# The second pair row of one token tile, moved to GpSimd at the end of a two-layer trunk

## The chip, the cores and the metric

The kernel runs on one core of a Trainium2 chip. A core has a matrix engine (TensorE, PE in the profile), a vector engine (VectorE, DVE), a scalar engine (ScalarE, ACT), GpSimd (POOL) and SyncE (SP), which only issues transfers. Each engine works through its own queue of instructions in program order, and semaphores hold an instruction back until others have finished. The metric is the device time of one execution in microseconds (us), lower is better. A few runs of the same kernel lie between 996.86 and 999.53 us.

## What is computed

256 latent tokens and 256 context tokens of width 1024 pass through two layers; each has a mixer and a mixture of experts with 32 experts, of which every token uses two. In the second ("odd") layer only the latent tokens are computed to the end. The change touches the last step of that layer, the sum over the two experts of each token, and what follows it:

```python
# top-2 experts of the chosen group, weights top_w
def add_expert(acc, p):
    w1_e, w3_e, w2_e, c_e = p
    hidden = jax.nn.silu(t @ w1_e) * (t @ w3_e)
    return acc + c_e[:, None] * (hidden @ w2_e), None
...
x = x + mx[5] * hierarchical_moe(hx, *moe_p)     # mx[5]: the gate
return rmsnorm(x, norm_final)
```

For a token with experts a and b this is x + w_a·g·y_a + w_b·g·y_b, and then a norm over the row.

## The kernel before

**Experts.** The 32 experts run one after the other, each on up to 64 gathered token rows (CAP = 64). TensorE makes a hidden layer (L1256), turns it (L1266) and multiplies it down to 1024 columns (L1282), which stand in PSUM as two halves of 512 columns on 64 partitions each. In the odd layer VectorE multiplies the result by the gate into the tile `YS` (L2439, in RH), and GpSimd scatters the rows by an indirect transfer to `pair_out` in HBM (L2844). There every token has two rows, one for its first and one for its second expert.

**Late experts.** The results of the last two experts (`LATE`, 30 and 31) don't take the way through HBM in the odd layer. Their places in `pair_out` are filled with zeros early on, and TensorE adds their rows from `YS` to the tokens by a product with `late_T`, a table of weights built beforehand (L1380). The other results come back: when GpSimd has seen the scatters end, it raises `most_stored` (L2942), and SyncE issues four loads (L876) into `back[t]` (in RAB), one for each tile t of 128 tokens and half h of 512 columns. Each counts on its own semaphore `y_back[t][h]`. A load of 512 KB brings both rows of the 128 tokens, first at `D*h` and second at `D*h + 512`.

**The end of the odd layer.** `LATE_TILES = (1, 0)`: tile 1 goes first, tile 0 is the second late tile. For each tile, TensorE (`late_results`) runs four late products (two experts, two halves; L1380) and then, for each half, one product of `first_weight[:, t, :]`, a diagonal matrix of the first expert's weights, with the first rows in `back` (L1385); it closes the PSUM bank of that half. An f32 product appears in the profile as two or more records. VectorE (`late_pair`) adds for each half the second rows times `topw[:, t, 1:2]` to the state X (L2498), and then the closed bank to X (L2505), which raises `x_updated`. ScalarE takes squares of the updated X (L1764) and a root (L1768); VectorE forms the reciprocal (L2194) and the normalised rows (L2198), and ScalarE's queue stores them (L2111). The helper `step` makes an instruction count on a semaphore of its engine and lets what follows on this engine wait for it.

**Order.** The queues follow the program: on VectorE, tile 1's two L2498, its two L2505, tile 0's two L2498, its two L2505, then the two final tiles. GpSimd has nothing to do after `most_stored` in the odd layer.

Of the kernel before, what the change touches and what calls it, by code (L numbers as in the profile page):

```python
# [19 lines left out]
ALU = mybir.AluOpType  # L20
# [4 lines left out]
D = 1024  # L25
# [281 lines left out]
LATE = (EXPERTS - 2, EXPERTS - 1)  # L307
LATE_TILES = (1, 0)
# [29 lines left out]
def trunk(nc, A):  # L338
# [6 lines left out]
    with ctx:  # L345
        def sb(name, shape, dt=F32):
            return ctx.enter_context(nc.sbuf_tensor(name, shape, dt))

        def sem(name):
            return ctx.enter_context(nc.semaphore(name))  # L350


        X = sb("X", [P, 4, D])
# [76 lines left out]
        back = [RAB[:, 0:2048], RAB[:, 2048:4096], RH[:, 2048:4096], RM[:, 0:2048]]  # L430
# [38 lines left out]
        topw = small[:, 152:160].rearrange("p (t k) -> p t k", t=4)  # L469
# [82 lines left out]
        first_hot_ready, first_full, first_ready = sem("first_hot_ready"), sem("first_full"), sem("first_ready")  # L552
        extra_ready, routed = sem("extra_ready"), sem("routed")
        rows_sent = sem("rows_sent")
        gidx_ready, sidx_ready = sem("gidx_ready"), sem("sidx_ready")
        gathered = [sem(f"gathered{i}") for i in range(4)]
        scattered = [sem(f"scattered{i}") for i in range(2)]
# [13 lines left out]
        y_back = [[sem(f"y_back{t}{h}") for h in (0, 1)] for t in range(4)]  # L571
# [39 lines left out]
        def full(eng, *name):  # L611

            eng.wait_ge(psum_full, plan[name]["full"])
            return bank_of(name)

        def drained(eng, *name):

            job = plan[name]
            eng.wait_ge(act_drained if job["who"] == "act" else dve_drained, job["drained"])
# [65 lines left out]
        def gate_loaded(eng, l, v):  # L685
            eng.wait_ge(ld_gate[l, v], 16 * (2 - l))

        def chained(eng, semaphore):

            count = [0]  # L690

            def step(ins, wait=True):
                count[0] += 1
                ins.then_inc(semaphore, 1)
                if wait:
                    eng.wait_ge(semaphore, count[0])

            step.sync = lambda: eng.wait_ge(semaphore, count[0])
            step.lag = lambda n: eng.wait_ge(semaphore, count[0] - n)
            return step  # L700
# [242 lines left out]
        def _(pe):  # L943
# [3 lines left out]
            def open_bank(*name):  # L947
                assert next(order) == name, name
                for before in plan[name]["before"]:
                    drained(pe, *before)  # L950
                return bank_of(name)

            def close(mm):
                mm.then_inc(psum_full, 1)
# [6 lines left out]
            def freed(mm):  # L961

                if free_due[0]:
                    mm.then_inc(ring_free, free_due[0])
                    free_due[0] = 0
# [243 lines left out]
            def experts(l):  # L1209
# [161 lines left out]
                def late_results():  # L1371

                    banks = {(t, h): open_bank("late", l, t, h) for t, h in LATE_BANKS}
                    pe.wait_ge(late_ready, l + 1)
                    for t in LATE_TILES:
                        for e, expert in enumerate(LATE):
                            pe.wait_ge(y_ready, n0 + expert + 1)
                            for h in (0, 1):
                                p = slice(CAP * h, CAP * (h + 1))
                                mm = pe.matmul(banks[t, h], late_T[p, t, e, :], YS[p, expert % 2, :],  # L1380
                                               start=(e == 0), stop=False)
                                freed(mm)
                        for h in (0, 1):
                            pe.wait_ge(y_back[t][h], 16 * (l + 1))
                            close(pe.matmul(banks[t, h], first_weight[:, t, :], back[t][:, D * h:D * h + 512],  # L1385
                                            start=False, stop=True))
# [22 lines left out]
                with pe.Fori(PEELED[l], LAST_GROUP) as i:  # L1409
                    c = extra_counts(pe, l, i)  # L1410
                    for q in range(PER_LOOP):
                        step(i, q, c[q])
                last_steps(extra_counts(pe, l, LAST_GROUP))
                late_results()

                pe.wait_ge(y_ready, n0 + EXPERTS)
# [37 lines left out]
            for c in range(NCH):  # L1454
                g = c % 4
                mm = pe.matmul(bank[32 * g:32 * g + 32, 0:BLK], shift32[:, c, :], first_w[:, c, :],
                               start=(c < 4), stop=(c >= 4))
# [7 lines left out]
            for ft in (0, 1):  # L1465
                mm = pe.matmul(bank[:, 8 * ft:8 * ft + 8].rearrange("p (j s) -> p j s", j=4), shift_rows[:, P * ft:P * (ft + 1)],
                               ident.rearrange("p (j k) -> p j k", j=4)[:, :, 0:2], start=True, stop=True)
# [4 lines left out]
            for c in range(4):  # L1472
                mm = pe.transpose(bank[:, 40 * c:40 * c + 37], chan_rows[0:37, P * c:P * (c + 1)], ident[0:37, 0:37])
# [165 lines left out]
            in1 = {(what, b): at["in1", i] for i, (what, b, _) in enumerate(ODD_BLOCKS)}  # L1639
# [58 lines left out]
            for g in (0, 1):  # L1698
                bank = open_bank("DT", g)
                for n in range(4):  # L1700
                    pe.wait_ge(o_scaled, 4 * g + n + 1)
                    mm = pe.transpose(bank[:, P * n:P * (n + 1)], OD[:, 4 * g + n, :], ident)
# [412 lines left out]
        def _(dve):  # L2115
            step = chained(dve, dve_step)

            def done(ins):
                ins.then_inc(dve_drained, 1)
# [370 lines left out]
            def late_pair(l):  # L2490


                for t in LATE_TILES:
                    if l == 1:
                        for h in (0, 1):
                            half = slice(512 * h, 512 * (h + 1))
                            dve.wait_ge(y_back[t][h], 32)
                            step(dve.scalar_tensor_tensor(out=X[:, t, half], in0=back[t][:, D * h + 512:D * (h + 1)],  # L2498
                                                          scalar=topw[:, t, 1:2], in1=X[:, t, half],
                                                          op0=ALU.mult, op1=ALU.add))  # L2500
                    for h in (0, 1):
                        half = slice(512 * h, 512 * (h + 1))
                        bank = full(dve, "late", l, t, h)
                        if l == 1:
                            dve.tensor_tensor(X[:, t, half], X[:, t, half], bank, ALU.add).then_inc(x_updated, 1)  # L2505
                            continue
                        b = back[t][:, D * h + 512:D * (h + 1)]
                        dve.wait_ge(y_back[t][h], 16)
                        done(dve.scalar_tensor_tensor(out=b, in0=b, scalar=topw[:, t, 1:2], in1=bank,
                                                      op0=ALU.mult, op1=ALU.add))  # L2510
                        drained(dve, "late", 0, t, h)
                        gate_loaded(dve, 0, 5)
                        step(dve.tensor_tensor(b, b, G[:, t // 2, half], ALU.mult))
                        dve.tensor_tensor(X[:, t, half], X[:, t, half], b, ALU.add).then_inc(x_updated, 1)
# [158 lines left out]


            late_pair(0)
            for t in (1, 0):
                normed_tile(2, t)
# [110 lines left out]
        def _(pool):  # L2788
            step = chained(pool, pool_step)
# [24 lines left out]
            def experts(l):  # L2814
# [21 lines left out]
                def scatter(i, q):  # L2836
                    n, b = i * PER_LOOP + (n0 + q), q % 2
                    pool.wait_ge(y_ready, n + 1)
                    e = i * PER_LOOP + q
                    col = idx[:, 0, 1, e:e + 1] if isinstance(e, int) else idx[:, 0, 1, bass.ds(e, 1)]  # L2840
                    pool.tensor_copy(SIDX[b], col).then_inc(sidx_ready, 1)  # L2841
                    pool.wait_ge(sidx_ready, n + 1)
                    pool.sem_inc(pool_passed, 1)
                    pool.indirect_dma_start(out=pair_out[l], out_offset=bass.IndirectOffsetOnAxis(ap=SIDX[b], axis=0),  # L2844
                                            in_=YS[:, b, :], in_offset=None, bounds_check=4 * tokens[l] - 1,
                                            oob_is_err=False).then_inc(scattered[b], 16)
# [11 lines left out]
                def stored(x):  # L2858

                    with pool.If(x > 0):  # L2860
                        pool.wait_ge(x_scattered, x * 16)
# [78 lines left out]
                    pool.wait_ge(scattered[b], 16 * ((n0 + EXPERTS) // 2 - 1))  # L2940
                stored(pool.snap(extras))
                pool.sem_inc(most_stored, 1)  # L2942
                if l == 0:
                    for t in LATE_TILES:
                        for h in (0, 1):
                            pool.wait_ge(y_back[t][h], 16)
                    for q in (PER_LOOP - 2, PER_LOOP - 1):
                        scatter(LAST_GROUP, q)
                    for b in (0, 1):
                        pool.wait_ge(scattered[b], 16 * EXPERTS // 2)  # L2950
                    pool.sem_inc(pairs_stored, 1)
# [42 lines left out]
```

## Time and profile before

| | |
|---|---|
| median of 3 runs | 997.68 us (996.86 to 999.53) |
| the profiled execution, its time | 997.07 us |
| the profiled execution, its span in the trace | 995.3 us |
| TensorE busy, share of the span | 934.7 us, 94% |
| VectorE | 427.9 us, 43% |
| ScalarE | 247.2 us, 25% |
| GpSimd | 224.5 us, 23% |
| mean granted TensorE clock | 0.993 of full speed |

The profile comes from one execution; its own time is 1.8 us above the span of its instructions. Times in the rows below count from the span's start. The busy shares are means over all stages; the change lies in the last 14 us alone, and is read from there.

### The profile page before, as it was taken

What the parts mean: (1) busy time and instruction counts of PE and PEld (TensorE: products, weight loads), DVE (VectorE), ACT (ScalarE), POOL (GpSimd) and SP (SyncE); (2) the same over time, 40 slices, a digit from 0 to 9 for tenths busy, and PEclk for the clock granted to TensorE, in tenths of its full rate; (3) what the DMA queues carried; (4) which work ended last, traced back from release to release, by engine and by line L of the source; (5) the groups of instructions that cost most, each with busy time, mean ns of one, the idle gap of its engine ahead of it and who ended that gap; (6) DMA issues with size and microseconds to landing.
All of it is one profiled execution on the core that took longest, in us unless ns stands there. A gap on an engine that the chain in (4) does not pass through costs nothing.

```text
span 995.3 us, 17268 instructions
## 1 busy us (share of the span) xinstructions
PE 934.7 (94%) x5873; PEld 591.6 (59%) x5874; DVE 427.9 (43%) x906; ACT 247.2 (25%) x538; POOL 224.5 (23%) x309
## 2 busy tenths in 40 slices
PE   4999999999998899997988999999988999999986
PEld 3444448657886455554555565887875555555552
DVE  4399995577446011110111589556344222222224
ACT  4220102465243122221222340133143111111112
POOL 1017801110003333332431000000003343333310
PEclk9999999999999999999999999999999999999999
DMA  9979325899357899999999999883558999999996
GB/s 346 391 198 376 98 72 197 252 307 390 131 184 244 328 405 405 407 406 407 407 406 407 326 387 388 282 315 107 196 185 283 400 400 408 405 399 401 403 405 240
DMA packets 129948, 315.86 MB, mean 317 GB/s; under 512 B 28987, under 2 KB 60755, under 8 KB 129860
## 3 DMA queue, kind: packets, MB, share of 16 engines
q1 hardware_dynamic: 114152, 295.93, 79.9%
q0 software_dynamic: 10800, 12.72, 3.7%
q10 hardware_dynamic: 4908, 6.03, 1.7%
q8 instruction: 57, 0.93, 0.4%
q14 instruction: 31, 0.25, 0.1%
HBM read 315.00 MB, written 22.31 MB: 339 GB/s over the span
## 4 chain that ended last, share of the span: by engine, by line
PE 75%; DMA 12%; DVE 4%; issue 3%; SPq 2%; ACT 2%; POOLq 0%; DVEq 0%; POOL 0%; ACTq 0%
PE ps L1256 19%; PE ps L1056 17%; DMA ring<-in_moe_w 10%; PE ps L1282 9%; PE ps L1108 8%; PE ps L1066 6%; PE ps L1224 3%; PE ps L980 2%; PE ps L1266 2%; PE ps L1434 1%; DMA RH<-hrow,sidx_all 1%; SPq L765 1%; DMA mod_rows<-in_norm_ffn 1%; PE ps L1485 1%; PE ps L1516 1%
## 5 line engine op out<-in xcount | busy, mean ns | idle before, releaser
L1256 PE MATMUL ps<-ring,RT 128*64 128x256 f32 x2096 | 250.8, 387 | 17.3 <-DMA ring<-in_moe_w 14.8
L1256 PEld LDWEIGHTS ps<-ring,RT 128*64 128x64 f32 x2096 | 156.5, 139 | 84.4 <-issue 18.2
L1056 PE MATMUL ps<-RT,ring 128*128 128x512 f32 (+1 forms) x544 | 182.1, 493 | 1.1 <-DVE RT L2532 1.1
L1056 PEld LDWEIGHTS ps<-RT,ring 128*128 128x128 f32 x544 | 102.2, 190 | 77.2 <-issue 70.6
L2409 DVE TENSOR_TENSOR RT<-RT,ps 64x256 f32<-64x256 f32 x64 | 27.0, 423 | 257.1 <-ACT RT L1859 139.0
L1282 PE MATMUL ps<-ring,RT 128*64 128x512 f32 x424 | 100.3, 593 | 2.2 <-DVE RT L2415 1.8
L1859 ACT ACTIVATE RT<-ps 64x256 f32<-64x256 f32 x64 | 24.2, 378 | 242.9 <-PE ps L1256 221.9
L2579 DVE SCALAR_TENSOR_TENSOR RAB<-RM,chan,RAB 128x512 f32<-128x512 f32 x120 | 82.3, 766 | 0.0
L2844 POOL DMA_INDIRECT pair_out<-RH,sidx_all x62 | 63.2, 1019 | 55.4 <-POOL sidx_all L2841 51.7
L2820 POOL DMA_INDIRECT RH<-hrow,idx x7 | 7.8, 1120 | 288.6 <-DMA hrow<-RH 189.1
L2832 POOL DMA_INDIRECT RH<-hrow,sidx_all x56 | 59.3, 1060 | 49.4 <-issue 29.0
L1224 PEld LDWEIGHTS ps<-const,RH 128*128 128x128 f32 x252 | 35.0, 208 | 48.6 <-issue 48.6
L1853 ACT ACTIVATE RT<-ps 128x512 f32<-128x512 f32 x64 | 38.2, 597 | 74.1 <-PE ps L1224 70.0
L1066 PE MATMUL ps<-ring,RT 128*128 128x256 f32 x256 | 56.0, 380 | 0.0
L1282 PEld LDWEIGHTS ps<-ring,RT 128*64 128x64 f32 x424 | 31.3, 137 | 39.6 <-issue 30.7
L1066 PEld LDWEIGHTS ps<-ring,RT 128*128 128x128 f32 x256 | 48.5, 190 | 8.0 <-issue 1.6
L2415 DVE COPY RT<-ps 128x128 f32<-128x128 f32 x64 | 18.7, 291 | 75.9 <-PE ps L1266 70.4
L2958 POOL TENSOR_TENSOR RM<-RM,PR 128x512 f32<-128x512 f32 x4 | 33.6, 8421 | 71.8 <-ACT PR L1738 71.8
L1224 PE MATMUL ps<-const,RH 128*128 128x128 f32 x252 | 46.5, 307 | 2.2 <-issue 1.2
L2841 POOL COPY sidx_all<-idx 128x1 int32 (+1 forms) x62 | 11.5, 186 | 147.9 <-ACT RH L1868 67.3
L1108 PE MATMUL ps<-ring,RT 128*128 128x256 f32 x192 | 43.2, 381 | 0.9 <-ACT RT L1738 0.9
L1108 PEld LDWEIGHTS ps<-ring,RT 128*128 128x128 f32 x192 | 36.0, 190 | 7.2 <-issue 1.4
(325 smaller groups left out, 1061.6 us busy)
## 6 DMA issues: line engine op xcount, KB each, us to landing
ring<-in_moe_w SPq DMA_DIRECT2D x354, 512.0 KB
ring<-in_w_mod SPq DMA_DIRECT2D x96, 512.0 KB
ring<-in_odd_w_in SPq DMA_DIRECT2D x24, 512.0 KB
ring<-in_even_w_in SPq DMA_DIRECT2D x20, 512.0 KB
ring<-in_even_w_out SPq DMA_DIRECT2D x8, 512.0 KB
RAB<-in_moe_w SPq DMA_DIRECT2D x8, 512.0 KB, 7.4
RAB<-pair_out SPq DMA_DIRECT2D x8, 512.0 KB, 8.4
ring<-in_odd_w_out SPq DMA_DIRECT2D x8, 512.0 KB
```

The costliest lines, as they stand in the source:

```text
L1056: mm = pe.matmul(bank, w[:, c, P * ft:P * (ft + 1)], moving[:, c, :], start=(c == 0), stop=(c == NCH - 1))
L1066: mm = pe.matmul(bank[:, BLK * i:BLK * (i + 1)], chunk_of(c, t), w[:, c, :], start=(c == 0), stop=(c == NCH - 1))
L1108: mm = pe.matmul(bank[:, BLK * (b % 2):BLK * (b % 2 + 1)], source[:, c % 4, P * t:P * (t + 1)], w[b][:, c, :], start=(c == 0 and b % 2 == ...
L1224: mm = pe.transpose(ps[:, b, P * j:P * (j + 1)], XG[:, q % 4, j:512:4], ident)
L1256: mm = pe.matmul(bank[CAP * k:CAP * (k + 1), 0:BLK], xt(c), rows_at(w[k], c), start=(c == 0), stop=(c == NCH - 1))
L1282: mm = pe.matmul(bank[CAP * k:CAP * (k + 1), :], ht(f), w[:, D * f + 512 * k:D * f + 512 * (k + 1)], start=(f == 0), stop=(f == 1))
L1853: act.activation(XT[:, b, :, :, :].rearrange("p j a s -> p (j a s)"), ps[:, bank, :], ACT.Copy).then_inc(xT_ready, 1)
L2409: dve.tensor_tensor(HID[:, b, :], SA[:, b, :], ps[CAP:P, 2 + b, 0:BLK], ALU.mult).then_inc(hid_ready, 1)
L2579: return dve.scalar_tensor_tensor(out=out, in0=z, scalar=chan[:, ct, k:k + 1], in1=out, op0=ALU.mult, op1=ALU.add)
L2832: pool.indirect_dma_start(out=XG[:, q % 4, :], out_offset=None, in_=hrow[l], in_offset=bass.IndirectOffsetOnAxis(ap=GIDX[q % 4], axis=0), ...
L2844: pool.indirect_dma_start(out=pair_out[l], out_offset=bass.IndirectOffsetOnAxis(ap=SIDX[b], axis=0), in_=YS[:, b, :], in_offset=None, boun ...
L2958: pool.tensor_tensor(z, z, SG[:, ct % 2, :].rearrange("p (s t) -> p s t", s=2), ALU.mult).then_inc(gated_in, 1)
```

## The change

For tile 0 of the odd layer, and for nothing else:

- TensorE leaves out the two diagonal products; the late products of the last expert close the banks.
- GpSimd, after `most_stored`, waits for each half's load, multiplies the second rows in place by their weight and adds them to X; the addition raises the new semaphore `second_added`.
- VectorE's scaled addition (now L2508) takes the first rows (k = 0) in place of the second, and waits for `second_added` too.

Tile 1 stays as it was, and so does the even layer.

```diff
+        second_added = sem("second_added")
...
+                                last = (l, t) == (1, LATE_TILES[1]) and e == len(LATE) - 1
                                 mm = pe.matmul(banks[t, h], late_T[p, t, e, :], YS[p, expert % 2, :],
-                                               start=(e == 0), stop=False)
-                                freed(mm)
+                                               start=(e == 0), stop=last)
+                                if last:
+                                    close(mm)
+                                else:
+                                    freed(mm)
+                        if (l, t) == (1, LATE_TILES[1]):
+                            continue
                         for h in (0, 1):
                             pe.wait_ge(y_back[t][h], 16 * (l + 1))
                             close(pe.matmul(banks[t, h], first_weight[:, t, :], back[t][:, D * h:D * h + 512],
...
+                        k = 1 if t == LATE_TILES[0] else 0
                         for h in (0, 1):
                             half = slice(512 * h, 512 * (h + 1))
                             dve.wait_ge(y_back[t][h], 32)
-                            step(dve.scalar_tensor_tensor(out=X[:, t, half], in0=back[t][:, D * h + 512:D * (h + 1)],
-                                                          scalar=topw[:, t, 1:2], in1=X[:, t, half],
+                            if k == 0:
+                                dve.wait_ge(second_added, h + 1)
+                            step(dve.scalar_tensor_tensor(out=X[:, t, half], in0=back[t][:, D * h + 512 * k:D * h + 512 * (k + 1)],
+                                                          scalar=topw[:, t, k:k + 1], in1=X[:, t, half],
                                                           op0=ALU.mult, op1=ALU.add))
...
                 pool.sem_inc(most_stored, 1)
+                if l == 1:
+                    t = LATE_TILES[1]
+                    for h in (0, 1):
+                        half = slice(512 * h, 512 * (h + 1))
+                        pool.wait_ge(y_back[t][h], 32)
+                        second = back[t][:, D * h + 512:D * (h + 1)]
+                        step(pool.tensor_scalar(second, second, topw[:, t, 1:2], None, ALU.mult))
+                        pool.tensor_tensor(X[:, t, half], X[:, t, half], second, ALU.add).then_inc(second_added, 1)
```

At the end of TensorE's queue, after tile 1's late products, stood before (semaphores waited for in brackets; `y_back10` is tile 1, half 0):

```order
L1385 MATMUL ps<-RAB,BIAS 128x512 [waits y_back10]
L1385 MATMUL ps<-RAB,BIAS 128x512 [waits y_back11]
L1380 MATMUL ps<-RH,BIAS 128x512 [waits y_ready]
L1380 MATMUL ps<-RH,BIAS 128x512
L1380 MATMUL ps<-RH,BIAS 128x512 [waits y_ready]
L1380 MATMUL ps<-RH,BIAS 128x512
L1385 MATMUL ps<-RAB,BIAS 128x512 [waits y_back00]
L1385 MATMUL ps<-RAB,BIAS 128x512 [waits y_back01]
```

and now, with the diagonal products at L1392 and the late ones at L1382:

```order
L1392 MATMUL ps<-RAB,BIAS 128x512 [waits y_back10]
L1392 MATMUL ps<-RAB,BIAS 128x512 [waits y_back11]
L1382 MATMUL ps<-RH,BIAS 128x512 [waits y_ready]
L1382 MATMUL ps<-RH,BIAS 128x512
L1382 MATMUL ps<-RH,BIAS 128x512 [waits y_ready]
L1382 MATMUL ps<-RH,BIAS 128x512
```

Tile 0's two diagonal products are gone; nothing else on TensorE moved.

On VectorE, from tile 1's second scaled addition to the first final tile, stood before:

```order
L2498 SCALAR_TENSOR_TENSOR X<-RAB,small,X 128x512 [waits y_back11,dve_step]
L2505 TENSOR_TENSOR X<-X,ps 128x512 [waits psum_full,dve_step]
L2505 TENSOR_TENSOR X<-X,ps 128x512 [waits psum_full]
L2498 SCALAR_TENSOR_TENSOR X<-RAB,small,X 128x512 [waits y_back00]
L2498 SCALAR_TENSOR_TENSOR X<-RAB,small,X 128x512 [waits y_back01,dve_step]
L2505 TENSOR_TENSOR X<-X,ps 128x512 [waits psum_full,dve_step]
L2505 TENSOR_TENSOR X<-X,ps 128x512 [waits psum_full]
```

and now:

```order
L2508 SCALAR_TENSOR_TENSOR X<-RAB,small,X 128x512 [waits y_back11,dve_step]
L2515 TENSOR_TENSOR X<-X,ps 128x512 [waits psum_full,dve_step]
L2515 TENSOR_TENSOR X<-X,ps 128x512 [waits psum_full]
L2508 SCALAR_TENSOR_TENSOR X<-RAB,small,X 128x512 [waits second_added,y_back00]
L2508 SCALAR_TENSOR_TENSOR X<-RAB,small,X 128x512 [waits second_added,y_back01,dve_step]
L2515 TENSOR_TENSOR X<-X,ps 128x512 [waits psum_full,dve_step]
L2515 TENSOR_TENSOR X<-X,ps 128x512 [waits psum_full]
```

The instructions and their places are the same; tile 0's two scaled additions each wait for GpSimd as well.

GpSimd's queue ended with the wait for the scatters; behind it stands now:

```order
L2870 UNCONDITIONAL_BRANCH [waits x_scattered]
L2959 TENSOR_SCALAR RAB<-RAB,small 128x512 [waits y_back00]
L2960 TENSOR_TENSOR X<-X,RAB 128x512 [waits pool_step]
L2959 TENSOR_SCALAR RAB<-RAB,small 128x512 [waits y_back01]
L2960 TENSOR_TENSOR X<-X,RAB 128x512 [waits pool_step]
```

Four instructions are added there; each addition waits for the scaling ahead of it (`pool_step`).

## Rows read from the trace of the kernel before

**Rows 1.** Chain of work that ended last, the end: start us, us, what.

```profile
981.34 1.92 PE ps L1380 x8
983.26 1.91 PE ps L1385 x4
985.17 1.92 PE ps L1380 x8
987.09 1.93 PE ps L1385 x4
989.04 0.04 DVE X L2505
...
991.36 0.75 DVE RH L2198
```

**Rows 2.** Timeline of VectorE from 981 us: start, us, engine, line, operation, tiles, count.

```profile
981.99 1.53 DVE L2498 SCALAR_TENSOR_TENSOR X<-RAB,small,X 128x512 f32<-128x512 f32 x2
984.42 1.48 DVE L2505 TENSOR_TENSOR X<-X,ps 128x512 f32<-128x512 f32 x2 [0.90 <-PE ps L1385]
985.82 1.53 DVE L2498 SCALAR_TENSOR_TENSOR X<-RAB,small,X 128x512 f32<-128x512 f32 x2
988.25 1.48 DVE L2505 TENSOR_TENSOR X<-X,ps 128x512 f32<-128x512 f32 x2 [0.90 <-PE ps L1385]
```

**Rows 3.** Timeline of TensorE, its last two groups, tile 0.

```profile
985.11 1.99 PE L1380 MATMUL ps<-RH,BIAS 64*128 64x512 f32 x8
987.02 1.98 PE L1385 MATMUL ps<-RAB,BIAS 128*128 128x512 f32 x4
```

**Rows 4.** Timeline of ScalarE, the first squares of tile 0.

```profile
988.98 0.63 ACT L1764 ACTIVATE RAB<-X 128x512 f32<-128x512 f32 x1 [1.70 <-DVE X L2505]
```

**Rows 5.** Loads of L876, second and third, then third and fourth: starts, landing times.

```profile
L876 SPq DMA_DIRECT2D RAB<-pair_out x2: 431/432/434, 974.0 to 974.4; - x2
...
DMA to landing us min/median/max: 7.8/8.2/8.6
```

```profile
L876 SPq DMA_DIRECT2D RAB<-pair_out x2: 431/432/432, 974.4 to 974.9; - x2
...
DMA to landing us min/median/max: 8.6/9.0/9.3
```

**Rows 6.** Timeline of GpSimd: last instruction, then two-input additions, then one-input masks.

```profile
967.22 0.98 POOL L2844 DMA_INDIRECT pair_out<-RH,sidx_all  x1 [0.86 <-POOL sidx_all L2841]
```

```profile
61.90 4.31 POOL L2958 TENSOR_TENSOR RM<-RM,PR 128x512 f32<-128x512 f32 x2 [56.84 <-ACT PR L1738]
```

```profile
81.18 28.16 POOL L2958 TENSOR_TENSOR RM<-RM,PR 128x512 f32<-128x512 f32 x1 [14.97 <-ACT PR L1738]
```

```profile
109.30 1.18 POOL L2958 TENSOR_TENSOR RM<-RM,PR 128x512 f32<-128x512 f32 x1
110.43 0.45 POOL L2801 TENSOR_SCALAR_AFFINE_SELECT BIAS<-BIAS 64x288 f32<-64x288 f32 x1
111.03 0.45 POOL L2803 TENSOR_SCALAR_AFFINE_SELECT BIAS<-BIAS 64x288 f32<-64x288 f32 x1
```

```profile
112.23 0.71 POOL L2803 TENSOR_SCALAR_AFFINE_SELECT BIAS<-BIAS 64x288 f32<-64x288 f32 x1
...
154.34 2.50 POOL L2963 TENSOR_TENSOR RM<-RAB 128x512 f32<-128x512 f32 x2 [31.16 <-DVE RAB L2579]
```

**Rows 7.** Timeline of VectorE beside those GpSimd instructions.

```profile
59.39 7.90 DVE L2164 SCALAR_TENSOR_TENSOR RH<-ring,csilu,RH 128x1024 f32<-128x1024 f32 x5
```

```profile
78.40 29.90 DVE L2579 SCALAR_TENSOR_TENSOR RAB<-RM,chan,RAB 128x512 f32<-128x512 f32 x45
108.21 1.01 DVE L2143 SCALAR_TENSOR_TENSOR mod_rows<-ps,small,mod_rows 128x256 f32<-128x256 f32 x2
```

```profile
154.11 0.69 DVE L2603 TENSOR_TENSOR ps<-ps,BIAS 128x512 f32<-128x512 f32 x1
154.84 1.23 DVE L2604 TENSOR_REDUCE small<-ps 128x2 f32<-128x1024 f32 x1
```

**Rows 8.** Groups by line and shape on GpSimd: count, busy us, mean ns, idle before.

```profile
L2851 POOL MEMSET RH<- 128x512 f32 x2 | 1.1, 548 | 0.0
```

## Prediction

> **What bounds the kernel now.** I read the chain of work that ended last first, and only its end, since nothing before the loads of L876 is touched. From 981.34 us it runs through TensorE alone: late products of tile 1, its diagonal products, late products of tile 0, its diagonal products, about 1.92 us each, until VectorE adds the last bank to X [rows 1]. Then comes the tail: squares and root on ScalarE, reciprocal and scaled rows on VectorE, the store [rows 1, 4]. The timeline of VectorE says how much room there is beside that chain. Before each pair of L2505 it stood idle for 0.90 us with TensorE as releaser; tile 0's scaled additions ran from 985.82 to 987.35, and the bank addition had to wait until 988.25 [rows 2]. So the diagonal products of tile 0 sit on the path, and behind them VectorE has 0.90 us of slack, no more. GpSimd's last instruction ended at 967.22 + 0.98 = 968.2 us [rows 6]: it is free.
>
> **The change part by part.** *Removed:* tile 0's diagonal products, 1.98 us of TensorE [rows 3]. Their banks now close when the late products end, at 985.11 + 1.99 = 987.10 us [rows 3]. The full 1.93 us of the chain isn't the gain, because VectorE is late next: tile 0's scaled additions end at 987.35 at the earliest, and the bank addition then starts there in place of 988.25 [rows 2]. That caps the gain at 0.90 us. Everything behind (ScalarE's squares at 988.98, the two final tiles, the stores) hangs on tile 0's L2505 and moves with it one for one [rows 1, 4].
>
> *Unchanged in cost:* VectorE's two scaled additions of tile 0 read the first rows in place of the second, the same 128x512 shape from the same load, 1.53 us for two or some 0.75 us each [rows 2].
>
> *Added:* four GpSimd instructions in one queue, two scalings and two additions, and a wait of each of VectorE's two scaled additions for the GpSimd addition of its half. Queued behind that wait on VectorE are tile 0's bank additions and both final tiles, so nothing can go around it. GpSimd's own waits hold nobody else, as its queue ends there, and `most_stored` is raised ahead of them, so the loads start as before.
>
> When GpSimd can start: tile 0's loads are the third and fourth. The third was issued at 974.4 and landed 8.6 us later, at 983.0; the fourth at 974.9 and 9.3 us, at 984.2 [rows 5].
>
> What its instructions cost: the addition has rows of its own shape. Undisturbed it took 1.18 us, and 2.50 us for two, 1.25 each, beside VectorE instructions that take one input from SBUF or none [rows 6, 7]. I take 1.22. A scaling of 128x512 isn't in the trace. From below it is bounded by a memset of that shape, 0.55 us, which reads nothing [rows 8]; from above by the one-input mask of 288 columns in 0.45 us, which grows with the columns to 0.45 x 512 / 288 = 0.80 us [rows 6]. I take 0.65, in the middle. Between two GpSimd instructions of which the second waits for the first stand 111.03 - 110.88 = 0.15 us [rows 6]. So each half costs 0.65 + 0.15 + 1.22 = 2.02 us, and both 4.04 us.
>
> Where it meets VectorE: a GpSimd addition that began beside the convolution's scaled additions took 28.16 us; it ended at 109.34, 1.04 us after the run of 45 such VectorE instructions had at 108.30, which is about one addition's own time [rows 6, 7]. Those VectorE instructions have two inputs in SBUF, as L2498 has; the one that followed had one input in PSUM, as L2505 has, and didn't hold it up. Beside longer two-input instructions two additions took 4.31 us, 2.15 each [rows 6, 7]. So I count that the two engines exclude each other where VectorE runs a scaled addition, whichever began first, and not where it adds a bank.
>
> The Trainium skill says as much on the page "SBUF — State Buffer", section "Who interferes with whom": a VectorE instruction with two SBUF inputs and a GpSimd instruction that reads SBUF share one port pair, and the later one blocks until the first has finished. The trace bears it out with the 28.16 us; the rule speaks against this change, and with it the sum below comes to a loss, without it to a small gain (the second rival).
>
> The sum, in the trace's times. Load at 983.0, but VectorE is in tile 1's second scaled addition until 981.99 + 1.53 = 983.52 [rows 2]. GpSimd's first half: 983.52 + 2.02 = 985.54; VectorE's tile 1 additions of banks run beside it undisturbed to 985.90. GpSimd goes on with the scaling of half 1 from 985.54 to 986.19. VectorE, ready for tile 0's first scaled addition at 985.82 as before, finds the port taken, runs from 986.19 to 986.94, and now GpSimd's second addition, ready at 986.34, has to wait for it: 986.94 + 1.22 = 988.16. VectorE sees the semaphore some 0.04 us later and runs its second scaled addition to 988.95. The bank addition starts at about 988.97, against 988.25 before: **0.7 us later**.
>
> Ends of this sum: with scaling 0.80 and addition 1.25 the same steps give 985.72, 986.52, 987.27, 988.52, 989.31, a loss of 1.1 us. With a scaling of 0.55, an addition of 1.18 and a start at the load, the first half ends at 984.88, the second scaling at 985.43; if the second addition then takes the port ahead of VectorE it ends at 986.76, VectorE's two scaled additions follow to 988.26, and the loss is nothing. So 0.0 to 1.1 us later, and I take 0.7, which the middle values give. The cover for GpSimd's first half is TensorE's work on both tiles, which ends at 987.10; without that cover each further us of GpSimd would be a us of the end, as the second half's already is.
>
> Against the profiled execution: 997.07 + 0.7 = 997.8 us. Its time lies 0.6 us under the median of the runs shown, so the median becomes 997.68 + 0.7 = **998.4 us**.
>
> **The rivals.** *GpSimd and VectorE don't hold each other up here, or GpSimd is quick.* Then GpSimd runs through from 983.0: with 2.02 us each half it ends at 987.05, VectorE's second scaled addition at 987.84, and the bank addition starts 0.4 us earlier than before; with the cheapest values, 983.0 + 0.55 + 0.15 + 1.18 = 984.88, again 1.88 to 986.76, the gain is 0.7. It gives 997.3 to 997.0 us on the median. For it: the masks beside the same kind of VectorE stream took 0.71 in place of 0.45 us, so one-input GpSimd instructions get through [rows 6]. Against it: the 28.16 us, and that the last three GpSimd instructions stand just where VectorE wants its scaled additions.
>
> *The engines trade the port at every instruction and GpSimd becomes the bound* (the other side). If all four instructions take the 2.15 us of the additions at 61.90 [rows 6], GpSimd ends at 983.0 + 4 x 2.15 + 0.30 = 991.9, VectorE's second scaled addition at 992.7, and the bank addition is 4.4 us late: 1002.1 us. It decides from the point where GpSimd's four instructions need more than about 7.3 us (then the loss passes 3 us). Against it: VectorE has no stream of two-input work here; it waits itself, and the port is free meanwhile.
>
> *The products weren't on the path, and nothing moves.* Against it speaks the 0.90 us idle with TensorE as releaser [rows 2]; it would need GpSimd to hit 988.25 by chance and gives 997.7 us, inside the forecast's bounds. I count it there.
>
> **How the numbers follow.** Forecast (0.0 to 1.1 us later): 0.71. No hold-up, 0 to 0.7 us earlier: 0.19. GpSimd the bound, some 4 us later: 0.07. Something that the sum doesn't hold and that moves the whole run the other way by over 3 us: 0.03; the cap of 0.90 us says that the change itself can't. A measurement of this kernel can tell about 0.3%, 3 us, from no change. The first two lie within that: 0.90. Slower by more: 0.07; faster by more: 0.03. The range: from the no-hold-up rival's 997.0 less 0.6 us to the forecast's upper end 998.8 plus 1.2 us, as single runs of one kernel lie 0.8 under and 1.85 us over their median: 996.4 to 1000.0. It leaves out the GpSimd-bound rival.
>
> **What would show it.** Right: in the timeline of GpSimd two scalings of 0.55 to 0.80 us and additions of 1.2 us, the last stretched or late by a VectorE scaled addition and ending at about 988.2; TensorE's last record at about 987.1; before tile 0's second scaled addition VectorE idle with GpSimd as releaser; the idle before tile 0's bank addition gone; the bank addition at about 989.0. The no-hold-up rival shows the same with GpSimd done by 987.1. The GpSimd-bound rival shows additions of 2 us or more and VectorE idle for 4 us. Wrong would be a first scaling far above 0.8 us, loads that land much later than 983.0 and 984.2, or a time under 996.4 us, which no step here can give.

## The result, and the profile after

The changed kernel takes 1000.98 us in the median of 11 runs (998.94 to 1003.74), the kernel before 997.68 (995.40 to 999.53, also 11 runs). The ratio is 1.0030 with a 95% interval of 1.0018 to 1.0041: 3.0 us slower, 1.8 to 4.1. A second comparison, among the experiments, gives 1.0026 (1.0012 to 1.0039). The forecast was 0.7 us slower, with 1000.0 us as the upper end of the range: the side was right, the size was not, and the time fell out of the range.

The profiled execution took 999.48 us with a span of 997.7 us, 2.4 us more than that of before. First the timeline of GpSimd (start, us, engine, line, operation, tiles, count, idle before and its releaser):

```profile
983.93 1.57 POOL L2959 TENSOR_SCALAR RAB<-RAB,small 128x512 f32<-128x512 f32 x1 [15.32 <-DMA RAB<-pair_out]
985.58 1.27 POOL L2960 TENSOR_TENSOR X<-X,RAB 128x512 f32<-128x512 f32 x1
986.84 1.56 POOL L2959 TENSOR_SCALAR RAB<-RAB,small 128x512 f32<-128x512 f32 x1
988.48 1.26 POOL L2960 TENSOR_TENSOR X<-X,RAB 128x512 f32<-128x512 f32 x1
```

The additions cost 1.27 us, little more than the 1.18 to 1.25 us in the rows of before [rows 6], but a scaling costs 1.57 us: more than an addition of two inputs. The timeline of VectorE in the same stretch:

```profile
983.03 0.75 DVE L2508 SCALAR_TENSOR_TENSOR X<-RAB,small,X 128x512 f32<-128x512 f32 x1 [0.15 <-DVE X L2508]
984.56 1.48 DVE L2515 TENSOR_TENSOR X<-X,ps 128x512 f32<-128x512 f32 x2 [0.78 <-PE ps L1392]
986.96 1.10 DVE L2508 SCALAR_TENSOR_TENSOR X<-RAB,small,X 128x512 f32<-128x512 f32 x1 [0.92 <-POOL X L2960]
989.87 0.75 DVE L2508 SCALAR_TENSOR_TENSOR X<-RAB,small,X 128x512 f32<-128x512 f32 x1 [1.81 <-POOL X L2960]
990.66 1.29 DVE L2515 TENSOR_TENSOR X<-X,ps 128x512 f32<-128x512 f32 x2
```

The last two idle entries before tile 0's scaled additions, 0.92 and 1.81 us, name GpSimd's addition as releaser. The idle of 0.90 us before tile 0's bank addition [rows 2] is gone, and the bank addition starts at 990.66. TensorE is done long before:

```profile
981.41 1.99 PE L1382 MATMUL ps<-RH,BIAS 64*128 64x512 f32 x8
983.33 1.99 PE L1392 MATMUL ps<-RAB,BIAS 128*128 128x512 f32 x4
985.24 1.99 PE L1382 MATMUL ps<-RH,BIAS 64*128 64x512 f32 x8
```

Its last record ends at 987.23. The chain that ended last, in its last part (start us, us, what), now runs from the loads into GpSimd, where that of before ran through TensorE [rows 1]:

```profile
974.89 8.94 DMA RAB<-pair_out
983.84 0.09 issue
983.93 1.58 POOL RAB L2959
985.51 0.07 issue
985.58 1.27 POOL X L2960
986.85 1.54 POOL RAB L2959
...
989.87 0.76 DVE X L2508
```

One measure serves for all runs below, since the start of the stage wanders by a few us from one execution to the next: **the stage**, from the start of tile 1's late products on TensorE to the start of tile 0's first bank addition on VectorE, both by the timelines. Before it is 988.25 - 981.27 = 6.98 us (the expectations say 6.91, with the chain's 981.34 as the start), after it is 990.66 - 981.41 = 9.25 us. The stage holds 2.27 us, what follows is of equal length, and the measured 3.0 us have that in their interval.

The mean granted clock fell from 0.993 to 0.989. About half of this lies in the tail behind the stage. The windows of before from 988.25 us and of after from 990.66 us, the last column but two being the clock:

```profile
988.25:995.30 7.05, 0.76 (x2) 0.00 (x0) 4.35 (x8) 2.04 (x6) 0.00 (x0) 0.77 0.40 149
```

```profile
990.66:997.70 7.04, 0.00 (x0) 0.00 (x0) 4.35 (x8) 2.03 (x6) 0.00 (x0) 0.50 0.40 149
```

TensorE has nothing to do there: 0.50 is the lower level, 1.2 GHz, in a tail in which it runs no product. Most of the rest lies in the last 49 us ahead of the stage, where TensorE still works, before and after:

```profile
932.00:981.34 49.34, 42.59 (x296) 25.25 (x292) 10.76 (x26) 7.23 (x14) 9.85 (x16) 1.00 1.03 405
```

```profile
932.00:981.41 49.41, 42.79 (x287) 25.53 (x287) 10.11 (x26) 7.16 (x14) 9.76 (x16) 0.97 1.03 402
```

The change touches nothing there, and such a dip isn't its own: a second profile of the kernel before, taken below, shows 0.66 from 952 to 957 us. Both profiles reach the stage nearly at the same time, 981.27 and 981.41 us, and while TensorE runs in the stage both show 1.00. So the clock doesn't explain the longer stage.

### The profile page after: what moved, and what is told of

The parts are those of the page before. It is cut to its first block, busy times and chain, and to the rows that moved or that the text cites. A ratio compares the mean times of both kernels' runs of the same rounds, so it can differ in the third digit from the quotient of the medians.

```text
span 997.7 us, 17265 instructions
## 1 busy us (share of the span) xinstructions
PE 935.4 (94%) x5869; PEld 593.2 (59%) x5870; DVE 427.9 (43%) x906; ACT 247.3 (25%) x538; POOL 230.1 (23%) x313
## 4 chain that ended last, share of the span: by engine, by line
PE 75%; DMA 12%; DVE 4%; issue 3%; ACT 2%; SPq 2%; POOL 1%; POOLq 0%; DVEq 0%; ACTq 0%
PE ps L1257 18%; PE ps L1057 17%; PE ps L1283 9%; DMA ring<-in_moe_w 8%; PE ps L1109 8%; PE ps L1067 6%; PE ps L1225 3%; PE ps L981 2%; PE ps L1267 2%; DMA RH<-hrow,sidx_all 1%; PE ps L1441 1%; DMA mod_rows<-in_norm_ffn 1%; SPq L766 1%; PE ps L1492 1%; DMA RAB<-pair_out 1%
```

## The experiments

Theory: GpSimd's four instructions, queued behind the third load, are late by their own price. Rivals: the engines hold each other up at a shared port; the change disturbs the whole run (layout, numbers of semaphores); the products were never worth anything.

**What the products are worth.** GpSimd's block and VectorE's waits for it are left out:

```diff
-                            if k == 0:
-                                dve.wait_ge(second_added, h + 1)
...
-                if l == 1:
-                    t = LATE_TILES[1]
...
-                        step(pool.tensor_scalar(second, second, topw[:, t, 1:2], None, ALU.mult))
-                        pool.tensor_tensor(X[:, t, half], X[:, t, half], second, ALU.add).then_inc(second_added, 1)
```

> The changed kernel with GpSimd's part and VectorE's wait for it left out: tile 0's second rows are not added at all. It shows what taking tile 0's diagonal products off TensorE is worth. Theory: VectorE's two scaled additions start right after tile 1's bank additions, stage 6.91 - 0.90 = 6.0 us, time 0.9 us under before. Rival (the change disturbs the whole run, by fewer products or another program layout): time 1 us or more over before in spite of the shorter stage. Rival (the products weren't on the path): stage 6.9 us.

Measured: stage 987.27 - 981.15 = 6.12 us, ratio 0.9995 (0.9983 to 1.0007), 0.5 us faster with 0 in the interval.

```profile
985.70 1.53 DVE L2506 SCALAR_TENSOR_TENSOR X<-RAB,small,X 128x512 f32<-128x512 f32 x2
987.27 1.29 DVE L2513 TENSOR_TENSOR X<-X,ps 128x512 f32<-128x512 f32 x2
```

VectorE runs through without idle time and is the bound, 0.86 us earlier than before. The cap that the prediction took from VectorE's slack, 0.90 us, holds; the products were on the path, by 0.86 us of the stage, which is less than the whole time can tell from no change.

**GpSimd without its scalings.**

```diff
-                        step(pool.tensor_scalar(second, second, topw[:, t, 1:2], None, ALU.mult))
```

> The changed kernel with GpSimd's two scalings left out, so that tile 0's second rows are added without their weight. The stage from the first late product to the first bank addition of tile 0 took 6.91 us before and 9.25 us with the change. Theory (the price of GpSimd's four instructions, 2 x (1.57 + 0.08 + 1.27) us behind the third load, is what is late): two additions of 1.27 us from the landing on, GpSimd done some 3.1 us earlier, VectorE bound again, stage 6.2 to 6.6 us, the time 0.3 to 0.7 us under that of before. Rival (the engines hold each other up at the shared port): the additions stretch or VectorE's scaled additions start late beside them, stage 7.4 us or more. Rival (the change disturbs the whole run): the time stays about 1 us or more over before although the stage is as short as in before.

Measured: stage 988.41 - 982.30 = 6.11 us, as without GpSimd; ratio 1.0008 (0.9997 to 1.0020).

```profile
984.12 2.79 POOL L2959 TENSOR_TENSOR X<-X,RAB 128x512 f32<-128x512 f32 x2 [15.29 <-DMA RAB<-pair_out]
```

```profile
986.85 1.53 DVE L2508 SCALAR_TENSOR_TENSOR X<-RAB,small,X 128x512 f32<-128x512 f32 x2
988.41 1.29 DVE L2515 TENSOR_TENSOR X<-X,ps 128x512 f32<-128x512 f32 x2
```

Two additions in 2.79 us are hidden wholly. It takes the scalings to make GpSimd late: with them the stage is 9.25 us, or 8.86 in the second profile of the change below. That 9.25 - 6.11 us equals 2 x 1.57 us is chance. The load came 0.7 us earlier here (GpSimd began 1.82 us behind the stage's start, 2.52 with the change), and the second addition ended some 0.7 us before VectorE needed it; the two cancel. The whole time didn't follow: 0.8 us over before (0.3 under to 2.0 over), where 0.3 to 0.7 under had been expected. The stage can't give that; it is taken up below.

**Is it the factor's operand, the operation, or the columns?** In place of the line taken out just above stands, in one kernel each, a scaling by a constant, a product of two tensors, and two pieces:

```diff
+                        step(pool.tensor_scalar(second, second, 0.5, None, ALU.mult))
```

```diff
+                        step(pool.tensor_tensor(second, second, topw[:, t, 1:2].broadcast_to([P, 512]), ALU.mult))
```

```diff
+                        for c in (0, 256):
+                            ins = step(pool.tensor_scalar(second[:, c:c + 256], second[:, c:c + 256], topw[:, t, 1:2], None, ALU.mult), wait=(c == 256))
```

> The changed kernel with GpSimd's scaling by the constant 0.5 in place of the column of weights, so the weight of tile 0's second rows is not applied. Theory (1.57 us is the price of this one-input operation as such): scaling 1.57 us, stage 9.25 us, time as with the change, some 2.4 us over before. Rival (reading the weight from SBUF costs): scaling 1.2 us or less, stage 8.5 us or less, time at most 1.6 us over before.

> The changed kernel with GpSimd's scaling written as a product of two tensors, the second rows and the column of weights spread over 512 columns. Theory (the operation with one input and a factor is dear on GpSimd, 1.57 us, dearer than a two-input one of 1.27 us): scaling 1.2 to 1.3 us, each half 0.3 us shorter, stage 9.25 - 0.6 = 8.65 us, time 1.8 us over before. Rival (a scaling pass of this size takes 1.57 us in whatever form): scaling 1.5 us or more, stage 9.2 us, time 2.4 us over before.

> The changed kernel with each of GpSimd's scalings in two pieces of 256 columns. Theory (the price grows with the columns): 0.8 to 0.9 us a piece, stage 9.3 to 9.5 us. Rival (a fixed price per instruction of this kind, such as a call that has to be set up): 1.1 us or more a piece, stage 10.5 us or more.

The timelines of GpSimd, first with the constant, then as a product of two tensors:

```profile
983.17 1.50 POOL L2959 TENSOR_SCALAR RAB<-RAB 128x512 f32<-128x512 f32 x1 [14.10 <-DMA RAB<-pair_out]
...
985.99 1.48 POOL L2959 TENSOR_SCALAR RAB<-RAB 128x512 f32<-128x512 f32 x1
```

```profile
984.38 1.13 POOL L2959 TENSOR_TENSOR RAB<-RAB,small 128x512 f32<-128x512 f32 x1 [15.23 <-DMA RAB<-pair_out]
...
986.82 1.04 POOL L2959 TENSOR_TENSOR RAB<-RAB,small 128x512 f32<-128x512 f32 x1
```

VectorE's first scaled addition of tile 0, which ran beside that second product:

```profile
986.96 1.44 DVE L2508 SCALAR_TENSOR_TENSOR X<-RAB,small,X 128x512 f32<-128x512 f32 x1
```

A single piece of 256 columns on GpSimd:

```profile
986.96 0.92 POOL L2960 TENSOR_SCALAR RAB<-RAB,small 128x256 f32<-128x256 f32 x1
```

With a constant 1.48 to 1.50 us, so reading the weight costs some 0.07 us and no more; stage 9.21 us, ratio 1.0023 (1.0011 to 1.0035). Written as a product of two tensors the same scaling takes 1.04 to 1.13 us, a third less and below the 1.2 to 1.3 expected; stage 990.44 - 982.36 = 8.08 us, of which the load gave 0.5 us by coming earlier (GpSimd began 2.02 us behind the stage's start); ratio 1.0022 (1.0011 to 1.0033). In pieces of 256 columns 0.92 us each, but for the first, which met a scaled addition of VectorE (2.15 us for it and the next); stage 9.37 us; there is one run, of 999.87 us. From 0.92 and 1.57 us the operation costs, by an estimate, 0.0025 us a column and 0.27 us beside. So the price belongs to the operation and grows with the columns; a fixed setup of a first call is excluded, as the second scaling costs as much as the first.

**GpSimd's work beside the kernel before, with nobody waiting.** The same four shapes, written into a free tile:

```diff
+        second_added = sem("second_added")
...
+                if l == 1:
+                    t = LATE_TILES[1]
+                    for h in (0, 1):
+                        pool.wait_ge(y_back[t][h], 32)
+                        second = back[t][:, D * h + 512:D * (h + 1)]
+                        aside = RM[:, 1024 * h:1024 * h + 512]
+                        step(pool.tensor_scalar(aside, second, topw[:, t, 1:2], None, ALU.mult))
+                        pool.tensor_tensor(RM[:, 1024 * h + 512:1024 * h + 1024], aside, second, ALU.add).then_inc(second_added, 1)
```

> The kernel before, with GpSimd's four instructions of the same shapes added, reading tile 0's second rows and writing into a free tile; nothing waits for them and TensorE keeps its products. Theory (only the wait for GpSimd costs): scaling 1.57 us, addition 1.27 us, stage 6.9 us, time as before. Rival (the shared port): tile 0's scaled additions on VectorE run later than 0.9 us, the stage grows to 7.5 us or more. Rival (GpSimd's work disturbs the run elsewhere): time 1 us or more over before with the stage unchanged.

Measured: stage 988.69 - 981.70 = 6.99 us, ratio 1.0011 (0.9998 to 1.0023).

```profile
986.74 2.00 POOL L2951 TENSOR_SCALAR RM<-RAB,small 128x512 f32<-128x512 f32 x1
```

```profile
986.25 2.15 DVE L2499 SCALAR_TENSOR_TENSOR X<-RAB,small,X 128x512 f32<-128x512 f32 x2
988.69 1.48 DVE L2506 TENSOR_TENSOR X<-X,ps 128x512 f32<-128x512 f32 x2 [0.29 <-PE ps L1386]
```

The engines do hold each other up: VectorE's two scaled additions take 2.15 us in place of 1.53, GpSimd's scaling 2.00 in place of 1.57. But 0.6 us of VectorE's slack of 0.90 us swallow it (0.29 us idle is left), and the stage doesn't grow.

**Other places for the scaling, or half of the work.** ScalarE scales, GpSimd only adds:

```diff
-        second_added = sem("second_added")
+        second_added, second_scaled = sem("second_added"), sem("second_scaled")
...
+            t = LATE_TILES[1]
+            for h in (0, 1):
+                act.wait_ge(y_back[t][h], 32)
+                second = back[t][:, D * h + 512:D * (h + 1)]
+                act.activation(second, second, ACT.Identity, scale=topw[:, t, 1:2]).then_inc(second_scaled, 1)
             combine_pair(1, 0)
...
-                        pool.wait_ge(y_back[t][h], 32)
+                        pool.wait_ge(second_scaled, h + 1)
...
-                        step(pool.tensor_scalar(second, second, topw[:, t, 1:2], None, ALU.mult))
```

> The changed kernel with the two scalings moved from GpSimd to ScalarE, which waits for the loads there; GpSimd only adds. Theory (GpSimd's scaling is the late part and ScalarE does it in some 0.65 us beside): GpSimd done by 6.0 us after the first late product, VectorE the bound, stage 6.1 to 6.7 us, time 0.2 to 0.8 us under before, which the timing can't tell from no change. Rival (ScalarE's squares of tile 1 are pushed back and the end with them): stage as short, but the end of the span less than 6.9 us behind it no longer holds, time 0.5 us or more over before.

Measured: ScalarE's scalings take 0.72 us each, and its first squares of tile 1 come behind them:

```profile
988.36 0.63 ACT L1771 ACTIVATE RAB<-X 128x512 f32<-128x512 f32 x1 [0.17 <-DVE X L2520]
```

They aren't held up: ScalarE stood idle for 0.17 us before them, until VectorE's bank addition released it, and they start 988.36 - 984.48 = 3.88 us behind the stage's start, as before (985.14 - 981.27 = 3.87). Stage 990.93 - 984.48 = 6.45 us; the rest of the span is 7.1 us, as before. The ratio is 1.0016 (1.0002 to 1.0030), 1.6 us over, and the stage says 0.5 us under. Its profile has lateness ahead of the stage, which starts at 984.48 us; but so it does in a profile of the kernel before taken again (984.67, below), so one execution tells nothing there.

Half 0 by GpSimd, half 1 by the diagonal product, VectorE taking half 1 first (the last two lines of the diff are GpSimd's loop); then the same with the scaling as a product of two tensors:

```diff
-                                last = (l, t) == (1, LATE_TILES[1]) and e == len(LATE) - 1
+                                last = (l, t) == (1, LATE_TILES[1]) and e == len(LATE) - 1 and h == 0
...
-                        if (l, t) == (1, LATE_TILES[1]):
-                            continue
-                        for h in (0, 1):
+                        for h in ((1,) if (l, t) == (1, LATE_TILES[1]) else (0, 1)):
...
-                        k = 1 if t == LATE_TILES[0] else 0
-                        for h in (0, 1):
+                        for h in ((0, 1) if t == LATE_TILES[0] else (1, 0)):
+                            k = 1 if t == LATE_TILES[0] or h == 1 else 0
...
-                    for h in (0, 1):
+                    for h in (0,):
```

> The changed kernel with the work split: half 0 of tile 0 goes by GpSimd as in the change, half 1 by the diagonal product and VectorE's second rows as before; VectorE takes half 1 first. Theory (one half costs GpSimd 2.92 us from the third load on, which ends beside TensorE's remaining work): VectorE's scaled addition of half 0 starts some 5.5 us after the first late product, stage 6.3 to 6.7 us, time 0.2 to 0.6 us under before. Rival (any wait for GpSimd on this path costs): stage 7 us or more, time over before.

> The version with the work split (half 0 by GpSimd, half 1 by the diagonal product), and GpSimd's scaling as a product of two tensors, which took 1.04 to 1.13 us in place of 1.57. Theory: GpSimd done some 0.5 to 0.9 us earlier than with the split alone, VectorE the bound, stage 6.1 to 6.2 us against 6.43 with the split alone and 6.98 before, time up to 0.9 us under before, which the timing can't tell from no change. Rival (something outside the stage costs every version about 1 us): time at or over before in spite of the shorter stage.

Split alone: stage 990.08 - 983.65 = 6.43 us, ratio 1.0003 (0.9991 to 1.0016). With the scaling as a product: stage 986.72 - 980.60 = 6.12 us, ratio 0.9996 (0.9987 to 1.0005).

```profile
982.27 1.48 POOL L2957 TENSOR_TENSOR RAB<-RAB,small 128x512 f32<-128x512 f32 x1 [14.69 <-DMA RAB<-pair_out]
983.83 1.28 POOL L2958 TENSOR_TENSOR X<-X,RAB 128x512 f32<-128x512 f32 x1
```

```profile
985.15 1.53 DVE L2506 SCALAR_TENSOR_TENSOR X<-RAB,small,X 128x512 f32<-128x512 f32 x2
986.72 1.49 DVE L2513 TENSOR_TENSOR X<-X,ps 128x512 f32<-128x512 f32 x2
```

GpSimd is done at 985.11, and VectorE, which takes half 1 first, needs half 0 only at 985.93; so it never waits, and the stage reaches the floor of 6.12 us that VectorE sets without any GpSimd. It undoes the loss of the change (ratio 0.9996 beside 1.0026 for the change in the same comparison, below). Whether it beats the kernel before can't be told: 0.86 us of the stage is less than the interval.

**Is there something outside the stage?** Three kernels in one comparison: before against itself, before with the new semaphore allocated and unused, and the change once more.

```diff
         rows_sent = sem("rows_sent")
+        second_added = sem("second_added")
```

> The kernel before, unchanged, measured against itself. Theory (the last stage holds the whole difference): ratio 1.000, its interval some 0.12% to either side, stage 6.98 us by the timeline's rows. Rival (kernels compared with before come out about 1 us late whatever they are): ratio about 1.001.

> The kernel before with the new semaphore allocated at its place and used by nothing, so that the semaphores behind it get other numbers. Theory (the last stage holds the whole difference): time as before, ratio 1.000, stage 6.98 us. Rival (the program's layout costs about 1 us outside the last stage): 1 us over before with the stage unchanged.

> The changed kernel once more, beside the null run and the semaphore alone, since its last stage grew by 9.25 - 6.98 = 2.27 us and its time by 3.0 (1.8 to 4.1) us. Theory (the stage holds it all): 2.3 us over before. Rival (another 1 us comes from the layout or from outside the stage): 3.3 us over before, and the two kernels beside it 1 us over too.

Before against itself: 1.0001 (0.9989 to 1.0013), stage 6.99 us. Semaphore alone: 0.9993 (0.9984 to 1.0002), stage 6.98 us. The change again: 1.0026 (1.0012 to 1.0039), 2.6 us, stage 990.86 - 982.00 = 8.86 us:

```profile
983.86 1.83 POOL L2959 TENSOR_SCALAR RAB<-RAB,small 128x512 f32<-128x512 f32 x1 [15.59 <-DMA RAB<-pair_out]
985.78 1.27 POOL L2960 TENSOR_TENSOR X<-X,RAB 128x512 f32<-128x512 f32 x1
987.03 1.56 POOL L2959 TENSOR_SCALAR RAB<-RAB,small 128x512 f32<-128x512 f32 x1
988.68 1.26 POOL L2960 TENSOR_TENSOR X<-X,RAB 128x512 f32<-128x512 f32 x1
```

```profile
990.07 0.75 DVE L2508 SCALAR_TENSOR_TENSOR X<-RAB,small,X 128x512 f32<-128x512 f32 x1 [1.81 <-POOL X L2960]
990.86 1.28 DVE L2515 TENSOR_TENSOR X<-X,ps 128x512 f32<-128x512 f32 x2
```

Neither the comparison itself nor the numbering of semaphores costs anything that can be told. **What stays open:** the stage grew by 1.9 and 2.3 us in the two profiles of the change, the times by 2.6 and 3.0. The difference of 0.7 us lies inside either interval. But the other versions lie above what their stage says too, counted from their ratios: by 2.1 us with ScalarE, 1.7 without the scalings, 1.1 with GpSimd aside and with the product, 0.9 with the split; others less, 0.5 with the split and the product, 0.4 without GpSimd, 0.1 with the constant. All have one sign, and the two kernels without any change of work don't show it (0.1 over and 0.7 under). For the version with ScalarE and the one without the scalings, what the stage says lies even outside the interval of the time (0.5 us under against 0.2 to 3.0 over, and 0.9 under against 0.3 under to 2.0 over). The part behind the stage, 7.0 to 7.1 us in their profiles as in before, doesn't hold the excess; ahead of the stage the profiles of one and the same kernel differ by 3.4 us (981.27 and 984.67), so single profiles can't show it. What added or missing instructions do to the program ahead of the stage, other than by the numbers of semaphores, was not varied by itself. Whether there is a small cost elsewhere stays open.

## Why the prediction was wrong, step by step

- *The products are on the path, and VectorE's slack caps the gain at 0.90 us* [rows 2]: right. The stage without GpSimd is 0.86 us shorter.
- *The step that failed is the price of the scaling.* It stood in the sum as 0.65 us, between a memset of 0.55 and a mask stretched by its columns to 0.80 us [rows 6, 8]. It took 1.57 us. The upper bound was no bound: the mask is another operation, on 64 partitions, and its 0.45 us for 288 columns say nothing of this one, which takes 0.92 us for 256. The rows held a nearer upper end in the other direction, a two-input addition of the same shape; even its 1.18 to 1.25 us would have been too little. Put the measured 1.57 us, and the 0.07 us seen between scaling and addition, into the prediction's own sum: 983.52 + 1.57 + 0.07 + 1.27 = 986.43 for half 0, 986.43 + 2.91 = 989.34 for half 1, 989.34 + 0.04 + 0.75 = 990.13 for VectorE and a bank addition at 990.15, 1.9 us behind the 988.25 of before. The second profile of the change has a stage 8.86 - 6.98 = 1.88 us longer. The term is mis-sized by 0.92 us, twice: 1.84 us, more than the 1.2 us by which this sum passes the predicted 988.97. The sum also held 0.60 us that didn't come, the hold-up of GpSimd's second addition (988.16 less 1.22 is 986.94, where it was ready at 986.34), and its other terms make up 0.06 us. So one error hid a part of the other, and it was luck that the forecast came no further from the result.
- *When the load lands:* 983.0 was forecast and 983.84 came. GpSimd began 2.52 us behind the stage's start, and 1.86 us in the second profile of the change, where its first scaling met VectorE and took 0.27 us longer (1.83). The rest of 0.66, 0.39 us, is what the first profile's stage is longer by. Before, this scatter was hidden by the 2.8 us between the third load and VectorE's use of it at 985.82 [rows 2, 5]; with the change it moves the end one for one.
- *The engines exclude each other:* half right. GpSimd instructions that meet a scaled addition of VectorE do grow (1.83 and 2.00 us in place of 1.57; 1.48 in place of 1.04), and a scaled addition that meets one takes 0.89 to 1.44 us in place of 0.75. But the price in the sum, 0.60 us on GpSimd, was wrong: VectorE's first scaled addition of tile 0 began 0.12 us after GpSimd's scaling, ended 0.34 us ahead of it and took 1.10 us; it wasn't held back until the scaling's end, and the scaling wasn't stretched (1.56 us). GpSimd's last addition met nothing. The rule of the Trainium skill, "SBUF — State Buffer", section "Who interferes with whom", that the port pair is an exclusive lock, is not what this row shows: held off until the scaling's end, the scaled addition would have taken 2.19 us. With the product form the row agrees with it better, though not wholly (the scaled addition took 1.44 us beside a product of 1.04 us, and held off to its end it would have taken 1.65).
- *What is late next:* right. VectorE waits for GpSimd's second addition (1.81 us idle), and the bank addition and both final tiles are queued behind that wait.
- *The rivals:* the no-hold-up one falls with the price of the scaling, though in the first profile of the change no GpSimd instruction was stretched, as it had said. The GpSimd-bound one came near in kind, since GpSimd does set the end, but by another mechanism: its four instructions take 5.8 us (983.93 to 989.74), not by trading the port at every instruction (2.15 us each), but by two dear scalings.
- *The range:* it took in the ends 0.55 and 0.80 us of the scaling as if they bounded it. Had the upper end been the 2.15 us of the slowest addition that wasn't starved, the same steps without hold-up would have put the bank addition 3.2 us late, and the range, with the 1.2 us for scatter, would have reached 1002 us.

## What to carry to other kernels

An operation that the trace doesn't show has no upper bound in rows of other operations on the same engine, even with fewer inputs: leave the range open to what an instruction of that engine and shape may cost, and ask from which price on the sign turns. Work moved to an idle engine has to fit between the data's arrival and its use; here that was 2.8 us for half 0 and the work on it was 2.9 us, and another 2.9 us for half 1 stood in the same queue. And where a wait for a transfer moves to the path's end, the scatter of its landing moves there with it.

## What the runs showed of the hardware

- On GpSimd a multiplication of 128x512 f32 by one factor per partition takes 1.57 us, by a constant 1.49, and as a product of two tensors, the factor spread over the columns, 1.04 to 1.13 us (1.48 us where it met a scaled addition of VectorE): the form with two inputs is the cheaper one. An addition of two full tensors takes 1.27 us.
- ScalarE scales the same tile in 0.72 us, VectorE scales and adds it in 0.75 us.
- VectorE's scaled addition beside a GpSimd scaling takes 1.10 us, beside a GpSimd product 1.44 us, alone 0.75 us; an addition of a PSUM bank takes 0.68 to 0.69 us beside GpSimd, as in before.
